# RWKV chunks in two parities on all four array quarters, a copy moved ahead of a wait, short MLP loops, moved fill steps and other value banks

## The reference, cut to what matters

```
def step(s, inp):                       # s: (value 64) x (key 64)
    r_t, w_t, k_t, v_t, a_t, b_t = inp
    sa = einsum('bhvk,bhk->bhv', s, a_t)
    s = s * w_t + outer(sa, b_t) + outer(v_t, k_t)
    o = einsum('bhvk,bhk->bhv', s, r_t)
    return s, o
```

## Time and profile before

| | |
|---|---|
| median of three runs | 2312.78 us |
| the profiled execution's own time | 2312.51 us |
| its span | 2310.7 us |
| mean granted clock | 0.995 |
| DVE, ACT, POOL busy | 43%, 18%, 24% |

### The profile page before, as it was taken

The page is one execution under the profiler, slowest core; times in us unless marked ns, Lnnn a source line. Parts: engine busy times, 40 slices in busy tenths (PEclk is TensorE's granted clock), DMA queues, the critical chain, the costliest instruction groups (busy, mean ns, idle before and its releaser), DMA issues.

```text
span 2310.7 us, 46981 instructions
## 1 busy us (share of the span) xinstructions
PE 2259.9 (98%) x20858; PEld 2143.1 (93%) x20858; DVE 987.0 (43%) x1259; ACT 420.1 (18%) x743; POOL 554.7 (24%) x288
## 2 busy tenths in 40 slices
PE   8999899999999999999999999999999999999998
PEld 6899888888888899979999988999999999999997
DVE  5333663746537445262544154454205313402523
ACT  4111313214132121153011032110000000000011
POOL 0222101102011022113333200333223323323331
PEclk9999999999999999999999999999999999999999
DMA  7211101102021065327113134111111111111112
GB/s 279 83 45 45 54 19 51 43 28 79 7 63 43 23 212 184 102 94 287 46 37 118 46 112 163 46 37 45 46 46 46 46 43 40 46 46 46 41 42 87
DMA packets 57738, 171.60 MB, mean 74 GB/s; under 512 B 8416, under 2 KB 24160, under 8 KB 54752
## 3 DMA queue, kind: packets, MB, share of 16 engines
q1 hardware_dynamic: 46816, 143.63, 18.4%
q10 hardware_dynamic: 10752, 25.35, 3.1%
HBM read 140.90 MB, written 28.05 MB: 73 GB/s over the span
## 4 chain that ended last, share of the span: by engine, by line
PE 88%; DVE 4%; DMA 2%; ACT 2%; issue 1%; SPq 1%; POOL 0%; ACTq 0%; DVEq 0%; POOLq 0%
PE ps L376 88%; DMA w_raw<-w 2%; DVE F L1092 1%; SPq L2126 1%; DVE TT L1092 1%; ACT F L1679 1%; DVE F L1095 0%; DVE F L1098 0%; ACT L1679 0%; DMA par<-par 0%; PE ps L950 0%; DVE Xst L1092 0%; POOL w_split L367 0%; ACT T L1679 0%; DVE attT L1547 0%
## 5 line engine op out<-in xcount | busy, mean ns | idle before, releaser
L376 PE MATMUL ps<-A_s,w_split 128*128 128x364 f32 (+1 forms) x6192 | 1082.0, 333 | 12.1 <-ACT zstg L1679 8.7
L376 PEld LDWEIGHTS ps<-A_s,w_split 128*128 128x128 f32 x6192 | 1029.4, 189 | 38.7 <-issue 13.2
L376 PE MATMUL ps<-B_s,w_split 128*128 128x364 f32 (+3 forms) x4032 | 672.4, 328 | 0.2 <-POOL w_split L367 0.2
L376 PEld LDWEIGHTS ps<-B_s,w_split 128*128 128x128 f32 x4032 | 667.7, 188 | 3.4 <-issue 1.0
L364 POOL CAST w_split<-w_raw 128x1024 fp32r<-128x1024 f32 x142 | 152.4, 1073 | 1710.3 <-PE ps L376 1626.0
L367 POOL TENSOR_TENSOR w_split<-w_raw,w_split 128x1024 fp32r<-128x1024 f32 x142 | 402.1, 2831 | 11.4
L1092 DVE TENSOR_TENSOR F<-ps,F 128x1092 f32<-128x1092 f32 (+3 forms) x52 | 62.8, 1208 | 420.6 <-PE ps L376 420.6
L1679 ACT ACTIVATE B_s<-T 128x1092 fp32r<-128x1092 f32 x32 | 35.9, 1120 | 622.7 <-DVE T L1098 622.7
L1098 DVE SCALAR_TENSOR_TENSOR T<-ps,rsx 128x1092 f32<-128x1092 f32 x32 | 41.5, 1296 | 206.4 <-PE ps L376 198.3
L1092 DVE TENSOR_TENSOR B_s<-T,B_s 128x1092 fp32r<-128x1092 f32 x32 | 105.9, 3309 | 1.1
L1092 DVE TENSOR_TENSOR T<-T 128x1092 f32<-128x1092 f32 x58 | 105.0, 1810 | 1.9 <-ACT T L1679 0.7
(11 more groups left out here) (208 smaller groups left out, 1901.9 us busy)
## 6 DMA issues: line engine op xcount, KB each, us to landing
w_raw<-w SPq DMA_DIRECT2D x144, 512.0 KB, 3.5
z<-zstg SPq DMA_DIRECT2D x83, 182.0 KB, 1.9
F<-z SPq DMA_DIRECT2D x16, 546.0 KB, 6.9
w_raw<-w SPq DMA_DIRECT2D x7, 1024.0 KB, 10.3
kc<-kc SPq DMA_DIRECT2D x7, 1024.0 KB, 4.9
vc<-vc SPq DMA_DIRECT2D x7, 1024.0 KB, 4.9
F<-x SPq DMA_DIRECT2D x8, 546.0 KB, 9.6
Zs<-z SPq DMA_DIRECT2D x16, 273.0 KB, 18.5
```

Source lines behind the costliest of these rows:

```text
L376: return pe.matmul(out, lhsT, rhs, start=start, stop=stop, skip_group_check=skip)
```

## The change

- The chunks of a batch are split by parity. Chunks 0 and 2 go through `both` into bank 3u, chunks 1 and 3 through `cross` into bank 3u+1, alternately, in `scores`, `turns`, `gq` and the inner products of the chain. In NAR, TK, WU and so on they then stand in the order of the products, and `begin`, `states`, `turned_square` and `out_read` read two banks at once. `begin` waits for all three parts of a batch's scores. The samples keep the old forms under new names.
- `chain`: the inner state products of all four chunks are issued together ahead of the steps (`state_products`), and so are the inner output products (`out_products`), which first wait until PE's own state products of the batch have landed (`tk_done`). A step of the chain is then one `sd` and one `oc`. Steps 2 of u = 0 and 0 to 2 of u = 1 have one fill step behind them (before: none), and the state products of u = 1 and output products stand in steps 0 and 1 of u = 0.
- `fill(22)` ahead of the first pair becomes fill(8), a mark, and fill(14), and ACT reads the side groups to this mark ahead of its wait for the mixed tile.
- The last `fill(3)` ahead of `r_var` becomes `fill(6)`. The cap of 768 stays, so later fills end sooner.
- `values(6)` goes to its score banks as well, without the wait; the first output unit waits for `at_of` 14 in place of 12.
- The MLP is eight loops of two units.

```
+            def products(out, u, terms, first):
+                for i in range(2):
+                    for k, (x, y) in enumerate(terms):
+                        both(out(u, 2 * i), x[:, i, :], y[:, i, :], start=(first and i == k == 0), stop=False, skip=True)
+                        last = cross(out(u, 2 * i + 1), x[:, 2 + i, :], y[:, 2 + i, :], start=(i == k == 0), stop=False, skip=True)
+                last.then_inc(tk_done, 1)
+            def out_products(p, u, n):
+                pe.wait_ge(tk_done, n)
+                products(oc_of, u, ...)
...
+            def chain(p, g, u, between):
+                h, n0 = 2 * g + u, turned_of(p, g)
                 for c in range(NB):
+                    n, j = h * NB + c, 2 * (c % 2) + c // 2
                     if n:
                         pe.wait_ge(s_ready, p * HALVES * NB + n)
+                    if c == 1:
+                        pe.wait_ge(tk_done, n0 + 4 + 2 * u)
+                    both(sd_of(u, c), G0T[u][:, j, :], Sst[:, n, :], start=False, skip=True).then_inc(s_done, 1)
+                    if c == 0 and u == 0:
+                        out_products(p, 0, n0 + 3)
+                    last = both(oc_of(u, c), Sst[:, n, :], QT[u][:, j, :], start=False, skip=True)
+                    if c == 0 and u == 0:
+                        state_products(p, h + 1, 1)
+                    elif c == 1 and u == 0:
+                        out_products(p, 1, n0 + 5)
+                    elif c < NB - 1:
+                        fill(between)
...
+            def scores(p, h, u):
+                for i in range(2):
+                    cross(inv[:, 1, i, :], Bbuf[:, e], Abuf[:, e])
+                    both(ps[:, b0, ...], Bbuf[:, e], F[:, 0:3:2, e])
+                    last = cross(inv[:, 0, 2 + i, :], Abuf[:, o], Bbuf[:, o])
...
-            fill(22)
+            fill(KT)
+            mark("mixing")
+            fill(14)
...
-                fill(3)
+                fill(3 if h < RH - 1 else 6)
...
-            return 4 if n < NA - 1 else score_banks(n)
+            return 4 if n < NA - 2 else score_banks(n)
...
+            for g in range(4):
+                plain(S_MLP + 16 * g, u + 16 * g, 8, A_s, hold=(h_ready, 18), skip=0 if g else 2)
+                plain(S_MLP + 16 * g + 8, u + 16 * g + 8, 8 if g < 3 else 6, B_s, hold=(up_s, g * 8))
...
-                    v.wait_ge(sc_done, 3 * q + k + 1)
+                        v.wait_ge(sc_done, 3 * q + 3)
...
+            load(A["o_sh"], nsh[:, :, :], d_nsh)
+            reads(MARK["mixing"])
+            a.wait_ge(pw_mixed, XT + 2)
```

More of the change, by code:

```diff
@@ L531, in scores, with sample_turns @@
                 last.then_inc(sc_done, 1)
-            def turns(p, h, u, nb):
+            def sample_turns(p, h, u, nb):
                 q, b0, cs = q_of(p, h), 3 * u, chunk_cols(h, nb)
@@ L581, in wu, with gq @@
                 last.then_inc(wu_done, 1)
-            def gq(p, h, u, nb):
+            def gq(p, h, u):
                 q, b0 = q_of(p, h), 3 * u
                 pe.wait_ge(wu_ready, q + 1)
[L586 to L589, removed]
-                last.then_inc(gq_done, 1)
@@ L592, in chain @@
[L592 to L601, removed]
+                for i in range(2):
+                    for k, x in enumerate((TK[u][:, 2, :, :], NAR[u][:, 0, :, C:2 * C])):
+                        d = slice(2 * C * k + C * i, 2 * C * k + C * i + C)
+                        both(ps[:, b0, d], WU[u][:, i, 0, :], x[:, i, :])
+                        last = cross(ps[:, b0 + 1, d], WU[u][:, 2 + i, 0, :], x[:, 2 + i, :])
@@ new lines, in gq, with sample_q_in, sd_of, oc_of @@
+                last.then_inc(gq_done, 1)
+            def sample_q_in(p):
+                q = q_of(p, HALVES)
+                pe.wait_ge(wu_ready, q + 1)
+                both(bank(0, 2, NB, C)[:, 1, 0, :], WU[0][:, 0, 0, :], NAR[0][:, 0, 0, C:2 * C]).then_inc(gq_done, 1)
+            def sd_of(u, c):
+                return ps[:, 3 * u + 1 + c % 2, C * (c // 2):C * (c // 2) + C]
+            def oc_of(u, c):
+                return ps[:, 3 * u + 2 - 2 * (c % 2), C * (2 + c // 2):C * (3 + c // 2)]
@@ new lines, in products, with state_products @@
+            def products(out, u, terms, first):
+                for i in range(2):
+                    for k, (x, y) in enumerate(terms):
+                        both(out(u, 2 * i), x[:, i, :], y[:, i, :], start=(first and i == k == 0), stop=False, skip=True)
+                        last = cross(out(u, 2 * i + 1), x[:, 2 + i, :], y[:, 2 + i, :], start=(i == k == 0), stop=False, skip=True)
+                last.then_inc(tk_done, 1)
+            def state_products(p, h, u):
+                pe.wait_ge(gq_ready, q_of(p, h) + 1)
+                products(sd_of, u, ((TK[u][:, 2, :, :], WU[u][:, :, 1, :]), (TK[u][:, 3, :, :], TK[u][:, 4, :, :])), True)
@@ L629, in group @@
                         pe.wait_ge(oc_ready, q_of(p, h - 2) + 1)
-                    scores(p, h, u, NB)
+                    scores(p, h, u)
                     fill(2)
                 for u in range(2):
-                    turns(p, 2 * g + u, u, NB)
+                    turns(p, 2 * g + u, u)
                 mark(p, g, "turned")
@@ L658, in samples @@
                 pe.wait_ge(oc_ready, q_of(p, 2) + 1)
-                scores(p, h, 0, 1)
+                sample_scores_in(p, h, 0, 1)
                 fill(3)
-                turns(p, h, 0, 1)
+                sample_turns(p, h, 0, 1)
                 mark(p, "s turned")
@@ L1025, in _ @@
             open_slot(S_CO)
-            pe.wait_ge(at_of, 2 * (NA - 2))
+            pe.wait_ge(at_of, 2 * (NA - 1))
             for c in range(3):
@@ L1232, in states @@
                 if nb == NB:
-                    own.add(tt(G0T[u][:, :, :], bank(b0, 2, NB, C)[:, 0, :, :], over(M_EYE, NB), ALU.add))
-                tt(QT[u][:, 0:nb, :], bank(b0, 2, NB, C)[:, 1, 0:nb, :], t1[:, cols].rearrange("p (c n) -> p c n", c=nb),
-                   ALU.add).then_inc(gq_ready, 1)
+                    own.add(tt(square(G0T[u][:, :, :]), ps[:, b0:b0 + 2, 0:2 * C].rearrange("p a (i n) -> p a i n", i=2),
+                               over_square(M_EYE), ALU.add))
+                    tt(square(QT[u][:, :, :]), ps[:, b0:b0 + 2, 2 * C:4 * C].rearrange("p a (i n) -> p a i n", i=2),
+                       t1[:, cols].rearrange("p (i a n) -> p a i n", i=2, a=2), ALU.add).then_inc(gq_ready, 1)
+                else:
+                    tt(QT[u][:, 0:nb, :], bank(b0, 2, NB, C)[:, 1, 0:nb, :], t1[:, cols].rearrange("p (c n) -> p c n", c=nb),
+                       ALU.add).then_inc(gq_ready, 1)
             def carry(p, h, u):
@@ L1784, in _ @@
             u += XT
[L1785 to L1793, removed]
             taken = [0]
@@ L1808, in reads @@
                     taken[0] += 1
+            load(A["o_sh"], nsh[:, :, :], d_nsh)
+            reads(MARK["mixing"])
+            a.wait_ge(pw_mixed, XT + 2)
+            own.add(act(xm[0:64, LORA_T, :], xm[0:64, LORA_T, :], ACT.Tanh))
+            own.add(act(xm[:, GL_T, :], xm[:, GL_T, :], ACT.Tanh, scale=0.5))
+            own.wait()
+            a.sem_inc(lora_act, 1)
+            a.wait_ge(d_nsh, 16)
+            a.wait_ge(d_x, 16 * 5)
+            a.sem_inc(nsh_ready, 1)
             def turned(p, h, u, nb):
@@ L1828, in out_read @@
                 a.wait_ge(oc_done, q + 1)
-                act(t1[:, cols].rearrange("p (c n) -> p c n", c=nb), bank(b0 + 2, NB, C)[:, 0:nb, :], ACT.Copy
-                    ).then_inc(oc_ready, 1)
+                if nb == NB:
+                    a.wait_ge(s_ready, (p * HALVES + h + 1) * NB)
+                    out = t1[:, cols].rearrange("p (i a n) -> p a i n", i=2, a=2)
+                    act(out[:, 0], bank(b0 + 2, 4, 2, C)[:, 1, :, :], ACT.Copy)
+                    act(out[:, 1], bank(b0, 4, 2, C)[:, 1, :, :], ACT.Copy).then_inc(oc_ready, 1)
+                else:
+                    act(t1[:, cols].rearrange("p (c n) -> p c n", c=nb), bank(b0 + 2, NB, C)[:, 0:nb, :], ACT.Copy
+                        ).then_inc(oc_ready, 1)
             load(lw[:, :], A["wda"][:, 0:P], d_lora)
```

91 lines of the change are left out of this document (58 added, 33 removed).

## The result

The changed kernel takes 2292.29 us (median of 4 runs, 2288.59 to 2293.93) against 2311.62 us for the kernel before on the same chip: ratio 0.9917, 95% interval 0.99 to 0.9935. The gain is 19.3 us, half of the 38 forecast. The profiled execution took 2292.49 us with a span of 2290.4 us at a granted clock of 0.996, so the spans differ by 20.3 us (2310.7 before).

A forecast was written before the change was run, and what follows sets the result against it. PE was taken as the bound, busy 98% of a 2310.7 us span. 2312.5 - 15.0 (groups) - 6.9 (ahead of first pair) - 12.6 (retention tail) - 3.2 (attention) - 0.9 (MLP) = 2273.9, so 2274 us; range 2262 to 2288.

The forecast's parts named there:

- where a weight slot begins: Groups: slots begin in the scores of three groups instead of two, POOL's split delaying DVE; +2.5 us with small change.
- Term A: Ahead of the first pair: with the copy ahead of the wait for xm, PE goes on; -6.9 us, bounds -5 and -8.5.
- A lone fill step costs 0.68 us here: Chain: 0.50 us for a fill step's matmuls and 0.18 for the change of shape; chain 7.1 us, 1.4 more.
- The fronts: Scores to first yz level, 8 groups: about 9.45 us against 12.1, gain 2.65 us a group.
- the place of the lora product: Ahead of the first pair: fill steps end at about 247.1, lora product at 247.5 us.
- the tail with its gap and low clock: End of retention: fewer fill steps, a new gap over 3 us, low clock adding 1.7; -12.6 us, bounds -17 and -9.
- the MLP loops: MLP: loops of two units remove the "issue" waits at jumps back; -0.9 us, bounds 0 and -1.5.
- gq: The gq products of each group: 0.47 us a batch against 0.94, giving 0.94 us a group.
- the wait of values(6): Attention: in the score banks no wait of 1.56 us and no low clock of 1.60; -3.2 us, bounds -1.5 and -4.
- term B: The eight groups with gq and chains: -15.0 us, bounds -24.5 (all of PE's saving comes through) and +26 (none).
- rival 2: The groups give nothing: DVE and POOL set the front, each chain step waits for DVE; 2289 us, chance 10%.
- rival 3: Tail without a clock drop and a microsecond less gap, POOL missing the groups; 2269 us, chance 12%.

The follow-up runs named there:

- x3: The changed kernel without the fill steps in the chains, its 32 steps going back to the tail of retention: 2292.74 us (ratio 0.9914).
- x5: The changed kernel with 12 fill steps, not 20, ahead of pair 1's lora product, 19 ahead of pairs 2 and 3's, 10 moved to retention's tail: 2284.12 us.
- x1: The changed kernel with POOL's subtraction done for one eighth of each tile from the third tile on: 2279.61 us (ratio 0.9862).
- x7: The changed kernel with the copy behind the mixing wait again, fill(22) in one piece: 2297.30 us (ratio 0.9947).
- x8: The changed kernel with scores, copies, gq and chain as before and no fill steps in the chains: 2303.59 us (ratio 0.997).
- x4: The changed kernel with two fill steps at each of four chain places in a pair's first group, none in its second: 2298.27 us (ratio 0.9945).
- x6: The changed kernel with ACT's last gated_hi ahead of its side reads after the last variance: 2296.19 us (ratio 0.9933).

## Why the prediction was wrong

- **The failed step: where a weight slot begins was counted for the groups alone.** "I put 1 us on each, with small change elsewhere, +2.5." The 32 steps in the chains shift every later slot, also in the stretches ahead of the scores, where DVE's chain of operations is long and PE soon waits for it: +4.1 us in pairs 1 and 2 and +1.9 in retention, where the forecast had nothing. Shown by x3 (no steps in the chains: both amounts are gone), x5 (same work, other places, -5.7 in three stretches) and x1. In the kernel before, pair 1's stretch showed it already: 30.46 us against 31.2 to 31.7 of the others.
- **Term A gave a third back.** It rests on ACT's first operation of the pair ("everything in pair 0 hangs on it"), which the forecast had at 249.1 in place of 256.04. It came at 250.22, behind squares that start at 248.66. So the lora product is 6.6 us earlier, but the stretch behind it grew by 2.2 (x7 and x8), and the pair's scores came 4.4 us earlier; 1.5 of the 2.2 is a low clock that came in five of the seven traces with this wait.
- The Trainium skill, SBUF — State Buffer (section "Who interferes with whom"), says that VectorE and GpSimd lock each other out of a shared pair of ports for a whole instruction, which touches DVE operations with two SBUF inputs or in a 2-port mode, and outside these modes none with at most one SBUF input. The trace agrees: in the first group, with POOL subtracting from 288.20 to 290.56, TT<-ps,msk (one input in PSUM) keeps its 0.43 us and TT<-TT,msk behind it takes 2.14, to 290.84. Two TENSOR_SCALAR with their one tensor input in SBUF took 2.80 us at 254.08 under POOL's subtraction, against 0.62 at 545.30; whether they ran in a 2-port mode, no row shows.
- **The mis-sized term: a fill step by itself in the chain.** "A lone fill step costs 0.68 us here": it is 0.84. I took the change of shape from the start of the first fill matmul to the next product, 0.18 us over 1.00; the 0.15 us ahead of that matmul had stood in the length of the scores. Four places a group at 0.16 are 0.64 us, which covers 7.7 against 7.1 and 5.1 of the 5.5 us that the eight groups are over here. x4 gives the same sizes.
- **The fronts:** 2.2 us a group where undisturbed (the second groups), not 2.65: there DVE starts 1.86 us after the scores and not 1.65, and ACT's copies end at 9.1, not 8.6. The three collisions came in the number forecast and cost 1.1 to 1.4 us each, not 1; pair 3's first front loses 1.0 us to "issue", PE waiting for nothing that the profile shows, and it stayed in x1. Together 4.9 us.
- **Right:** the place of the lora product (-6.6 for -6.9), the tail with its gap and low clock (-14.0 + 1.7 for -12.6), the MLP loops, gq (-0.92). In attention the wait of values(6) went as said, but PE is then early for the vc load: it waits for it twice, 2.2 us, where it waited once, 0.9 us, before; so -2.2 for -3.2.
- **A slip:** from its own terms the lower bound of term B is -24.2 and not -24.5; nothing hangs on it.
- **Rivals:** rival 2's mechanism, DVE and POOL setting the front, is the nearest, but the groups do give 4.6 us; rival 3, the tail without a clock drop, did not happen.

Open: what the "issue" wait in pair 3 is; why the rope stage takes 75.8 to 78.8 us in kernels with the same work there; and when the clock falls. Retention in x6 and x7 took 1.7 to 2.0 us more than in the changed kernel: in both the same wait of 2.4 us for S0r was followed by the low clock, in the changed kernel it was not. A single trace can therefore be off by some 1.5 us at each such wait.

## What to carry to other kernels

A filler that also opens weight slots carries a side effect: its position decides when another engine preprocesses the next weights. Before moving fill steps, list slot starts against the stages of the engine that shares ports with it; the places are free to choose, and here they were worth 5.7 us in three stretches. Price a filler from the last product before it to the first behind it, both changes of shape included, and look at what a fill step does for the clock as well as for time.

## What the hardware showed

POOL's subtraction on one eighth of a tile took 0.88 us in the mean against 2.8 for the whole. The clock did not go by the length of PE's wait. In the changed kernel waits of 2.29, 2.35 and 3.28 us were followed by 3.4 us at 1.2 GHz; those of 1.28 (to 1404.53), 1.85, 2.43 and 2.79 us (to 876.56) were not, and in the kernel before one of 1.56 us was the earlier trace rows. Nor did the same place always do the same: the 2.2 to 2.35 us in pair 0 were followed by it in five of seven traces, the 1.85 to 1.87 us in pair 1 in one of four (x4). Waits of 0.27 us in each step of a chain without fill steps were followed by it in 4 of 20 groups. A change from 64x64 to 128x128 products takes 0.15 to 0.20 us from start to start, the way back 0.26, against 0.16 between fill matmuls.
